# Query projections of a two-layer hybrid trunk in three passes of high and low parts, with the features split during layer 0's projections

## The reference

```python
h = x * (1.0 + sc1) + sh1                       # sc1, sh1: from silu(c) @ w_ada[l]
a_q, a_k, a_v, b_cq, b_ckv, b_kr, c_q, c_k, c_v, gate_logits = jnp.split(h @ w_in, offs, axis=-1)
...
g_a, g_b, g_c = jnp.split(jax.nn.sigmoid(gate_logits), N_BRANCHES, axis=-1)
p_a = o_a @ w_branch[:A_Q_W]                    # p_b, p_c alike
return (g_a * p_a + g_b * p_b + g_c * p_c) @ w_out
...
x = layer_norm(ALPHA * x + g1 * y, ln1_g[l], ln1_b[l])
h = x * (1.0 + sc2) + sh2
y = expert_choice_ffn(h, w_router[l], w_gate[l], w_up[l], w_down[l])   # 16 experts, each takes its 32 best tokens
x = layer_norm(ALPHA * x + g2 * y, ln2_g[l], ln2_b[l])
```

## Time and profile before

| | us |
|---|---|
| median of three runs (1727.95, 1731.94, 1732.47) | 1731.94 |
| profiled execution | 1731.32 |
| its span | 1729.1 |
| TensorE busy in the span | 1509.0 |
| VectorE busy | 506.7 |
| ScalarE busy | 399.4 |
| weights and inputs read | 520.04 MB, 302 GB/s mean |

### The profile page before, as it was taken

The page is one execution under the profiler, slowest core; times in us unless marked ns, Lnnn a source line. Parts: engine busy times, 40 slices in busy tenths (PEclk is TensorE's granted clock), DMA queues, the critical chain, the costliest instruction groups (busy, mean ns, idle before and its releaser), DMA issues.

```text
span 1729.1 us, 23510 instructions
## 1 busy us (share of the span) xinstructions
PE 1509.0 (87%) x9968; PEld 831.6 (48%) x9968; DVE 506.7 (29%) x1002; ACT 399.4 (23%) x860; POOL 23.2 (1%) x47
## 2 busy tenths in 40 slices
PE   6999998999999999899889899989997667776764
PEld 3544356888885343433222375578874233332322
DVE  0233666434462010011010364765630000000003
ACT  1222677222222011200000132854320001000000
POOL 1000000000000000000000100000000000000000
PEclk9999999999999999999999999999998678787777
DMA  9744931323459999999999941046899999999995
GB/s 366 269 168 197 421 110 62 116 79 116 191 205 346 423 421 420 421 421 420 422 421 421 335 153 47 3 148 192 349 415 421 421 420 421 420 421 420 421 421 227
DMA packets 101510, 522.71 MB, mean 302 GB/s; under 512 B 11024, under 2 KB 13344, under 8 KB 47136
## 3 DMA queue, kind: packets, MB, share of 16 engines
q1 hardware_dynamic: 97712, 509.97, 73.8%
q0 software_dynamic: 3392, 10.85, 1.9%
q10 hardware_dynamic: 304, 0.40, 0.1%
HBM read 520.04 MB, written 1.15 MB: 301 GB/s over the span
## 4 chain that ended last, share of the span: by engine, by line
PE 60%; DMA 18%; SPq 15%; DVE 5%; ACT 1%; issue 1%; DVEq 0%; ACTq 0%
PE psum L545 55%; SPq L1136 15%; DMA ring<-in_w_down 9%; PE psum L630 4%; DMA A<-in_w_down 3%; DMA ring<-in_w_up 3%; DMA ring<-in_w_gate 1%; DMA ring<-in_w_ada 1%; ACT hT L1284 1%; DVE X L1901 1%; DVE X L1791 0%; DVE X L1792 0%; DVE small L1761 0%; DVE PR L1780 0%; DVE small L1766 0%
## 5 line engine op out<-in xcount | busy, mean ns | idle before, releaser
L545 PE MATMUL psum<-ring,A 128*32 128x256 f32 (+1 forms) x2000 | 283.2, 541 | 70.1 <-DMA ring<-in_w_gate 35.8
L545 PE MATMUL psum<-ring_r,h_hi 128*128 128x512 f32 x704 | 219.9, 394 | 6.9 <-DVE h_lo L1798 5.8
L545 PEld LDWEIGHTS psum<-ring,A 128*32 128x32 f32 (+1 forms) x2000 | 92.2, 135 | 250.2 <-issue 112.0
L545 PE MATMUL psum<-A 128*32 128x256 f32 (+5 forms) x1056 | 168.1, 528 | 28.4 <-DMA A<-in_w_up 15.3
L1935 DVE TENSOR_TENSOR W<-W,psum 128x512 f32<-128x512 f32 (+1 forms) x32 | 17.7, 555 | 535.6 <-PE psum L545 535.6
L545 PE MATMUL psum<-ring,PR 128*32 128x256 f32 (+1 forms) x1056 | 145.4, 514 | 32.9 <-DMA ring<-in_w_down 32.9
L545 PE MATMUL psum<-ring,hT 128*128 128x512 f32 (+3 forms) x512 | 162.6, 471 | 3.4 <-issue 1.3
L545 PE MATMUL psum<-ring_r,h_lo 128*128 128x512 f32 x384 | 150.7, 393 | 0.0
L545 PEld LDWEIGHTS psum<-ring_r,h_hi 128*128 128x128 f32 x704 | 133.3, 190 | 35.6 <-issue 6.6
L545 PEld LDWEIGHTS psum<-ring,hT 128*128 128x128 f32 x512 | 85.0, 192 | 69.0 <-issue 66.7
L1522 ACT ACTIVATE W<-psum 128x512 f32<-128x512 f32 (+1 forms) x32 | 15.7, 490 | 426.2 <-PE psum L545 426.2
(11 more groups left out here) (206 smaller groups left out, 1453.6 us busy)
## 6 DMA issues: line engine op xcount, KB each, us to landing
ring<-in_w_down SPq DMA_DIRECT2D x91, 1024.0 KB, 26.7
ring<-in_w_gate SPq DMA_DIRECT2D x86, 1024.0 KB, 26.4
ring<-in_w_up SPq DMA_DIRECT2D x85, 1024.0 KB, 26.1
ring<-in_w_ada SPq DMA_DIRECT2D x40, 1024.0 KB, 14.3
ring<-in_w_in SPq DMA_DIRECT2D x36, 1024.0 KB, 5.1
A<-in_w_gate SPq DMA_DIRECT2D x36, 1024.0 KB, 24.3
A<-in_w_up SPq DMA_DIRECT2D x34, 1024.0 KB, 26.1
A<-in_w_down SPq DMA_DIRECT2D x26, 1024.0 KB, 26.4
```

The costliest lines, as they stand in the source:

```text
L545: return nc.tensor.matmul(o, a, b, start=start, stop=stop, skip_group_check=True)
```

## The change

- `KEPT`: slots 8 and 9 leave the ring of projections, attention and gates. `h_hi` lives there. For expert pieces they are used as before, A's `MID` and `HIGH` change places with them: these two are now filled at the end of attention (`load_early`).
- In layer 0 the four tiles of features are split during the projections: ScalarE does the high part i after the step that `QUERY_HIGH_AFTER` names, VectorE the low part after that of `QUERY_LOW_AFTER` (0 to 3 are tiles, 4 and 5 the two pieces of chunk 2, 6 and 7 those of chunk 0).
- In layer 0 chunks 2 and 0 are multiplied by `query_products`, in three passes: 8 matmuls become 24. The high parts of chunk 2 lie in A and PR (`query_hi`), those of chunk 0 in ring slots.
- The first four pieces of the third part of `w_ada` share the two slots that come free at that point, `ring_order[k % 2]`.
- More throwaway matmuls before the ranks (20 to 26), 5 inside the router's product of layer 1 and 3 instead of 7 before its last tile; in layer 1 ScalarE computes the next root between the two halves of a tile.

```diff
+KEPT = (8, 9)
-WARM_TURN, WARM_SCORE, WARM_CHOICE, WARM_RANKS, WARM_ROWS, WARM_TOKENS = 7, 3, 6, 20, 4, 20
+WARM_TURN, WARM_SCORE, WARM_CHOICE, WARM_RANKS, WARM_ROWS, WARM_TOKENS = 7, 3, 6, 26, 4, 20
+WARM_HALF, WARM_LAST = 5, 3
...
+QUERY_SPLITS = 8
+QUERY_HIGH_AFTER = {(1, 0): [0], (1, 1): [1], (1, 2): [2], (1, 3): [3], (3, 2): [4], (3, 3): [5], (2, 1): [6], (2, 2): [7]}
+QUERY_LOW_AFTER = {(3, 0): [0], (3, 1): [1], (3, 2): [2], (3, 3): [3, 4, 5], (2, 2): [6], (2, 3): [7]}
...
-AT_ONCE = {0: [ABOVE, BELOW, EARLY_B, LATE_B], 1: [ABOVE, BELOW, EARLY_B, LATE_B, MID, HIGH]}
+AT_ONCE = {0: [ABOVE, BELOW, EARLY_B, LATE_B], 1: [ABOVE, BELOW, EARLY_B, LATE_B, *KEPT]}
...
-        h_hi = fixed("h_hi", [P, KT, 512], F32R, "A", 4096)
+        h_hi = fixed("h_hi", [P, KT, 512], F32R, "ring", KEPT[0] * SLOT)
+        query_hi = [fixed("query_hi_a", [P, 4, 512], F32R, "A"), fixed("query_hi_p", [P, 4, 512], F32R, "PR")]
...
-        ring_order = list(range(RING))
+        ring_order = [s for s in range(RING) if s not in KEPT]
...
-            def load_tokens(l):
-
-                load_expert(l, filled_event(("hT", l, 1, 1)), TOKENS)
+            def load_early(l):
+
+                if l:
+                    load_expert(l, filled_event(("hT", l, 1, 1)), TOKENS)
+                for slot in (MID, HIGH):
+                    load_expert(l, filled_event(("O", l, 1, PAIR_ORDER[-1])), slot)
...
+            def mm3(o, a_hi, a_lo, b_hi, b_lo, first, last):
+
+                mm(o, a_hi, b_hi, first, False)
+                mm(o, a_hi, b_lo, False, False)
+                return mm(o, a_lo, b_hi, False, last)
...
-                n, w = piece(w_ada[l, k * P:(k + 1) * P, third * 2048:(third + 1) * 2048], 2048)
+                slot = ring_order[k % 2] if (l, third) == (0, 2) and k < 4 else None
+                if (l, third, k) == (1, 0, 0):
+                    ring_order[:] = ring_order[4:] + ring_order[:4]
+                n, w = piece(w_ada[l, k * P:(k + 1) * P, third * 2048:(third + 1) * 2048], 2048, slot=slot)
...
+            def query_products(ch, t):
+
+                if t == 0:
+                    if ch == 0:
+                        ring_order[:] = ring_order[2:] + ring_order[:2]
+                    a, w = CHUNKS[ch][0]
+                    query_held[ch] = [query_piece([w_in[0, 512 * i:512 * i + 512, a:a + w]], i if ch == 2 else None)
+                                      for i in (0, 1)]
+                b = begin(("P", 0, ch, t), takers=2 if ch != 0 else 1)
+                for i, (number, held, w_hi, w_lo) in enumerate(query_held[ch]):
+                    pe.wait_ge(split_low, split_base(0) + number)
+                    for k in range(4 * i, 4 * i + 4):
+                        cols = slice(t * P, (t + 1) * P)
+                        ins = mm3(psum[:, b, :], h_hi[:, k, cols], h_lo[:, k, cols], w_hi[:, k % 4, :], w_lo[:, k % 4, :],
+                                  k == 0, k == KT - 1)
+                event = end(ins, b)
...
                         wg = gate_pieces(n, br)
-                        for t in ts:
-                            h_split[t] = split_rows(l, hT, h_hi, h_lo, t)
+                        load_early(l)
+                        for t in ts if l else ():
+                            h_split[l, t] = split_rows(l, hT, h_hi, h_lo, t)
...
+                    if kind == "P" and l == 0:
+                        for i in QUERY_HIGH_AFTER.get(step[1:], ()):
+                            if i < 4:
+                                drained(act, ("hT", 0, i, 1))
+                            high(0, i)
...
+                    if kind == "P" and l == 0:
+                        for n in QUERY_LOW_AFTER.get(step[1:], ()):
+                            low(0, n)
```

More of the change, by code:

```diff
@@ L346, in first_splits, with early_splits @@
         def first_splits(l):
-            return 2 * len(tiles(l)) + 3
+            return (QUERY_SPLITS if l == 0 else 0) + 2 * len(tiles(l)) + 3 - (len(tiles(l)) if l == 0 else 0)
+        def early_splits(l):
+            first = QUERY_SPLITS if l == 0 else 0
+            return list(range(first, first + EARLY_SPLITS))
         def split_base(l):
@@ L362, in split_order @@
             for s in range(6):
-                before = list(range(EARLY_SPLITS, f)) if s == 0 else []
+                before = list(range(early_splits(l)[-1] + 1, f)) if s == 0 else []
                 after = []
@@ L417, in end, with piece @@
                 return (bank_filled[b], fills[b])
-            def piece(src, *shape):
-                n = load(src, *shape)
+            def piece(src, *shape, slot=None):
+                n = load(src, *shape, slot=slot)
                 pe.wait_ge(slot_filled[slot_of[n]], counts[n])
@@ L529, in split_piece, with query_piece @@
                 return len(splits[l]), n, hi, lo
+            def query_piece(src, i):
+                n = load(src, 4, 512)
+                m = take() if i is None else None
+                lo = part(ring_r[:, slot_of[n], :], 0, 4, 512)
+                hi = part(ring_r[:, slot_of[m], :], 0, 4, 512) if i is None else query_hi[i][:, :, :]
+                splits[0].append((pieces[n], hi, lo, hi.bitcast(F32), (n, m)))
+                return len(splits[0]), (n, m), hi, lo
             def split_rows(l, src, hi, lo, t):
@@ L886, in turn_tokens @@
                     if i == last or l:
-                        throw_away(WARM_TURN)
+                        throw_away(WARM_LAST if l and i == last else WARM_TURN)
                     pe.wait_ge(x_ready, 2 * first_tile(l) + i + 1)
@@ L1111, in _ @@
             step = QKV_TURNS
+            for t in tiles(0):
+                h_split[0, t] = split_rows(0, hT, h_hi, h_lo, t)
             for l in range(DEPTH):
@@ L1973, in _ @@
                 n_gates = 6 * first_tile(l)
-                for i in range(EARLY_SPLITS):
+                for i in early_splits(l):
                     low(l, i)
```

44 lines of the change are left out of this document (26 added, 18 removed).

## The result

The changed kernel takes 1735.23 us (median of nine runs, 1732.33 to 1741.37) against 1731.51 for the kernel before (nine runs, 1727.41 to 1734.61). The ratio of the runs is 1.0029, 95% interval 1.0017 to 1.0040: 5.0 us slower (2.9 to 6.9), while the two medians lie 3.7 us apart. That is right at the edge of what can be told apart, on the other side of the forecast of 1725.2, and above its range (1713 to 1732.5). The profiled execution took 1736.20 us, its span 1734.4 against 1729.1.

A forecast was written before the change was run, and what follows sets the result against it. TensorE was taken as the bound up to layer 1's experts, DMA transfers from 1230 us on. Terms -1.4 - 4.5 - 0.8 - 2.0 + 2.0 = -6.7 us took the median of 1731.94 to 1725.2 us, range 1713 to 1732.5.

The forecast's parts named there:

- Query products, -1.4: Layer 0, chunks 2 and 0: three passes save 12.2 us, waits before and in chunk 0 take most back; net -1.4 us.
- Gates of layer 0, -4.5: Start of layer 0's gates: features already split, so a 2.9 us wait and 1.7 us of lower clock go; -4.5 us.
- No cost: Layer 0's gates: first branch weights, behind two expert pieces, land near 290 for a product due at 299; no cost.
- Start of the gates, layer 1, +2.0, at most +6: Layer 1: branch rows land behind POOL's loads and two expert pieces, ready at 1150.2, needed at 1148.2; +2.0 us, ends 0 and +6.
- The sign that I gave for this term: Layer 1's gates: if the branch rows land after 1150, the last term (+2.0 us) is wrong.
- Stretch of transfers, -2.0: Layer 1's DMA stretch: early expert pieces leave one piece less to move; -2.0 us, ends 0 and -2.5.
- Ranks, -0.8: Ranks of both layers: six more throwaway matmuls may spare the lower clock that follows; -0.8 us, ends 0 and -1.6.
- second rival: "Nothing to be seen": chunk 0's waits eat all, gate starts give their lower ends; 0 to -3 us, 1730; chance 0.25.
- the low end of 1710.2: Past the range: the query term at its low end of -12.2 us, with -4.8, -1.6, -2.5 and 0 elsewhere.
- The third rival: Slower: SP's in-order queue delays weights at layer 0's chunk 0 and layer 1's gates; +9.0 us, 1740.9; chance 0.1.

The follow-up runs named there:

- e1: The changed kernel with the two early expert pieces issued behind the first branch rows in both layers; 1725.6 us, 0.9972 of the kernel before.
- e10: The changed kernel with the two early expert pieces issued behind the first branch rows in layer 1 alone; 1726.68 us, 0.9986 of the kernel before.
- e5: The changed kernel with POOL's four norm parameter loads in layer 1 held until ScalarE has cast the first branch rows; 1728.69 us, 0.9986 of the kernel before.
- e7: e4 with the throwaway matmul counts of the kernel before (20 at the ranks); 1718.54 us, 0.9931 of the kernel before.
- e8: e4 with A's MID and HIGH filled in layer 1 at the end of the gates, not of attention; 1719.85 us, 0.9938 of the kernel before.
- e9: e4 with the first token tile split before the second weight piece at layer 1's gates; 1715.17 us, 0.9916 of the kernel before.
- e4: The changed kernel with e1's edit, chunk 0's pieces issued before the modulation loads, and their splits one tile earlier; 1715.61 us, 0.9917 of the kernel before.

## Why the prediction was wrong

By its own terms, with the profiled executions for the sizes. The forecast was -6.7, the spans say +5.3, so 12.0 us are to be found. The step that failed is the start of layer 1's gates, mis-sized at +2.0 where it took 7.0; it makes up 5.0 of the 12.0, and the other steps the rest.

- *Query products, -1.4.* Right, -1.2: the last products of attention end at 276.04 instead of 277.2. The chain of reasons held link by link. Pieces forecast to land at 113.6 and 116.3 landed at 113.9 and 116.6; squares of tile 2 at 117.4, measured 117.22; the second half of chunk 0's first tile after a low part that ends at 132.6, measured 132.52. A tile in passes took 5.65 us (89.42 to 95.07) where I had 5.44. By four passes for a full product (the Trainium skill, "FP8 and Floating Point Precision", TensorE Precision Notes) an estimate is 5.2; the rows of the gates were the better guide. The clock's 1.7 us came as reckoned, and the first tile ended at 137.05 for 137.2.
- *Gates of layer 0, -4.5 and "No cost" for the branch rows.* -2.7. The wait and the low clock went, and 1.9 us came back inside the gates. What failed is the sentence that the rows, landing near 290 for a product due at 299, cost nothing. They did land at 292.65. But I looked only at the product that reads them and not at what is queued behind their cast on ScalarE; the table load and the sigmoids came late, and TensorE waited for banks. e1 against e10 gives 2.4 us for it, with an interval of the same size.
- *Start of the gates, layer 1, +2.0, at most +6.* The failed step: +7.0 in the trace, a wait of 5.35 us and 1.7 of lower clock, confirmed by e10 and e5, which undo it in two ways (7.4 us each by their ratios, 7.0 and 6.8 by their traces). The mechanism and the place were named; two terms of the size were wrong. First, the rows landed 13.5 us after the gates' start and not 10.2 (1145.8 against 1135.61 in the frame of the sum). I had taken POOL's loads at their old landing time and 2.5 us for each MB behind them. The second expert piece landed 9.9 us after the start (1142.7) for the 8.3 reckoned, since POOL's loads and the pieces were under way together and 290 GB/s moved over 1131 to 1135. The 0.75 MB of rows landed 3.6 us after it, where I had reckoned 1.9: they move at 224 GB/s. That is 3.3 us, and 2.0 + 3.3 is the wait that was seen. The product was due when I said, 12.8 us after the start for 12.6. Second, I had charged the lower clock for the wait in layer 0 but not for this one, 1.7 us. The sign that I gave for this term, rows landing after 1150, was of no use: they landed at 1146.3 (1149.1 in the frame of the sum), and the term was wrong all the same. What e1 adds is that the cost need not arise at all. The rows had lost a lead of 109 us over the gates, because two loads that wait stand ahead of them; I never looked up when the rows had been issued before.
- *Stretch of transfers, -2.0.* The stretch gave back 1.0. The other half, as I read it, went where the same two slots are missing, in the output projection's pieces: the route of layer 1, which I held at 0, took 1.2 us more.
- *Ranks, -0.8.* In the trace +0.5, since the lower clock came 15 us sooner in the execution seen; e7 can't tell what the counts are worth. Of the rest, the 0.9 in the tail goes with its lower clock, and 0.6 arose in the experts of layer 0, where the last piece on the chain took 29.34 us to land instead of 27.79.

The sum of the measured terms is -1.2 - 2.7 + 0.5 + 0.6 + 7.0 + 1.2 - 1.0 + 0.9 = +5.3, which is the difference of the spans. With layer 1's gates at the +2.0 forecast it would be +0.3: no loss, but no gain either. Two small slips of the recorded text changed nothing: the second rival's four numbers add up to +0.1, not to 0 to -3, and the low end of 1710.2 stands on the profiled execution, where the median would give 1710.8. The third rival, "one in-order queue holds the weights in both places", was the right kind of mechanism. I gave it 0.1, because I let it need a late landing of chunk 0 too, and because I set its place in layer 1 at a price below what it took. With the forecast for chunk 0 as it was, 7.0 us in layer 1 and the smaller gains elsewhere were enough.

## What to carry to other kernels

A load that waits, put ahead in an in-order queue, costs the loads behind it their whole lead, not the time of its bytes. So for each load in the old program behind the new place, look up when it used to be issued and when it will be now; the two expert pieces cost some 7 us in layer 1 in the wrong place (e10), and may be worth some 3.6 in the right one (e8, within the noise). Take the rate of a transfer from a row of the same shape, and charge each wait with the clock behind it. And of a late operand ask not only who reads it but what else stands behind the instruction that waits for it: both waits of this change in the gates were ScalarE's whole queue behind one cast, and e9's was one set further on.

## What was not expected of the hardware

- The branch rows (0.75 MB in two loads of 64 x 3 x 512) keep the DMA engines as busy as a 1 MB piece and move far less: 224 GB/s at a share of 1.05 in the change (1141 to 1146), 238 at 1.04 in e5 with POOL's loads out of the way, against 422 at 1.01 for expert pieces and 393 at 1.04 for the `w_in` pieces of e1 (1138 to 1143). What makes them slow no run shows. The share alone does not say how much arrives.
- The lower clock does not follow every wait. Behind the wait of 2.89 us at the start of layer 1's gates it was granted 0.66 over 5 us in the change and in e4, but 1.00 in e1 (1130 to 1135), and behind e9's wait of 3.11 us 1.00 as well (1132 to 1136). So its 1.7 us is a price that may or may not be paid.
- The low clock of the route moved: the same matmuls ran at 0.57 at 529 to 533 before, and in the changed kernel at 1.00 there and 0.54 at 511 to 516, with TensorE busy without a gap there. What the clock takes at one place can't be counted as saved when it is not seen there.
